# A transformer layer's expert stage: all products as three fp32r passes, row tile by row tile

## The chip, the core and the metric

The kernel runs on one core of a Trainium2 chip. The metric is the device time of one execution in microseconds (us). A core has TensorE (matmuls into PSUM), VectorE, ScalarE, GpSimd and the queues that issue DMAs; each engine works through its own instructions in order and waits on semaphores for the others. In profile rows they are PE, DVE, ACT, POOL and SP.

## The reference, cut to what matters

One layer of a hybrid attention and state-space trunk on 512 tokens of width 1024, then a mixture of experts, a gated embedding and a final norm. The change lies in the experts (and in the norm ahead of them):

```python
tok = h.reshape(-1, d)                         # h = rms_norm(x, moe_norm_w), 512 x 1024
logits = tok @ router_w + router_b             # 32 experts
top_vals, top_idx = lax.top_k(logits, 4)
gate_w = jax.nn.softmax(top_vals, axis=-1)
...
gu = lax.ragged_dot(x_sorted, w_up, group_sizes) + b_up[e_sorted]      # 1024 -> 2048
g, u = gu[:, :D_EXPERT], gu[:, D_EXPERT:]
g = jnp.minimum(g, 7.0)
u = jnp.clip(u, -7.0, 7.0)
act = (u + 1.0) * (g * jax.nn.sigmoid(1.702 * g))
out = lax.ragged_dot(act, w_down, group_sizes) + b_down[e_sorted]      # 1024 -> 1024
out = out * gate_w.reshape(-1)[order][:, None]
y = jax.ops.segment_sum(out, token_of, num_segments=n_tok)
```

Inputs and output are float32.

## The kernel before

The stages follow each other: projections, attention and the scan (to about 985 us), the router (to about 1085), the 32 experts (to about 2335), the gather of their outputs, the embedding and the final norm. All engines' programs are written out by hand, and their order is the order of the code; semaphores that only count up tie them.

An expert works on a block of 128 tokens. GpSimd gathers their rows from HBM (`fetch`, an index copy and an indirect DMA), TensorE transposes them (`turn_x`), VectorE multiplies the norm's weights in (`take_x`). The up product has 1024 rows of weights in eight row tiles of 128, and 2048 columns; it is made in two halves of 1024 columns, g and u of 512 each. Half 0 is plain fp32 products. Half 1 and the down product are made of three fp32r passes each (`mm3`): tokens and weights are split into a high part, which ScalarE writes (`ACT.Copy` into an fp32r tile, line 886), and a low part, which VectorE writes (the difference, line 1380), and the passes are high x high, high x low and low x high. The parts of one row tile of 1024 columns lie in one of four slots (`piece_hi`, `piece_lo`, in the trace `h_hi`, `h_lo`); a slot is written anew when TensorE has used it (`unit_used`). Tokens and activations are split in the same way (`x_hi`, `x_lo`, `act_hi`, `act_lo`, in the trace `w_hi`, `w_lo`).

After each up half VectorE clamps g and u out of PSUM, ScalarE takes the sigmoid of 512 columns, and VectorE joins them (`activate`, four VectorE operations of 512 columns). The activation is transposed (`turn_act`), split, and goes into the down product; ScalarE scales the result by the gate and stores it (`expert_out`, line 869). The experts overlap: a round b on TensorE is

```python
def round_of(b):
    up(b, 0)
    turn_act(b - 1)
    up(b, 1)
    turn_x(b + 1)
    down(b - 1)
```

Weights are loaded by SP: 16 loads of 512 KB for the up product and four of 1 MB for the down product, each when its place in SBUF has been read. The up loads have rows of 2 KB. All 32 experts' first blocks are computed; blocks for more than 128 tokens of an expert would follow, and none does here.

Of the kernel before, what the change touches and what calls it, by code (L numbers as in the profile page):

```python
# [15 lines left out]
P = 128  # L16
# [31 lines left out]
HALF = FF // 2  # L48
UNITS = 4
# [54 lines left out]
def up_piece(b, k):  # L104


    return b * 16 + (MOE_UNITS + k - (0 if isinstance(b, int) and b in (0, EXPERTS) else 8))


def down_piece(b, k):  # L110

    return b * 16 + (MOE_UNITS + k + (8 if isinstance(b, int) and b in (EXPERTS - 1, BLOCKS - 1) else 16))
# [30 lines left out]
def build(nc, x, p, mix_norm_w, w_in, lambda_q1, lambda_k1, lambda_q2, lambda_k2, da_head_norm_w,  # L143
# [3 lines left out]
    with ExitStack() as ctx:  # L147
# [32 lines left out]
        def bank(b, n=512, start=0):  # L180
# [126 lines left out]
        w_unit_up = [[arena[:, kb(32 * h + 8 * c):kb(32 * h + 8 * c + 8)].rearrange(  # L307
            "p (j u n) -> p j u n", j=2, u=2) for c in range(UNITS)] for h in range(2)]
        w_unit_dn = [at(64 + 8 * c, 2, D) for c in range(UNITS)]


        piece_hi, piece_lo = ([h[:, 2 * s:2 * s + 2, :] for s in range(4)] for h in (h_hi, h_lo))
        up_rows = [w_unit_up[1][k // 2][:, k % 2] for k in range(KT)]
        down_rows = [w_unit_dn[k // 2][:, k % 2, :].rearrange("p (n c) -> p n c", n=2) for k in range(KT)]
        act_hi, act_lo = w_hi[:, 0], w_lo[:, 0]
        x_hi, x_lo = w_hi[:, 1], w_lo[:, 1]
        xg, xgT = at(MOE_AT, D), at(MOE_AT + 4, KT, P)
        hidden = at(MOE_AT + 8, FF)
        y_out = at(MOE_AT + 16, D)
        g_sb, u_sb, sig_sb, t_sb = (at(MOE_AT + 20 + 2 * i, HALF) for i in range(4))  # L320
# [56 lines left out]
        (block_token_ready, xg_landed, x_turned, xt_ready, up_used, up_done, g_ready, sig_ready, hidden_own,  # L377
         act_ready, act_turned, actt_ready, act_hi_ready, x_hi_ready, x_lo_ready, down_done, y_ready, y_stored, bias_up_landed,
         bias_dn_landed) = (sem(n) for n in (
            "block_token_ready", "xg_landed", "x_turned", "xt_ready", "up_used", "up_done",  # L380
            "g_ready", "sig_ready", "hidden_own", "act_ready", "act_turned", "actt_ready",
            "act_hi_ready", "x_hi_ready", "x_lo_ready", "down_done", "y_ready", "y_stored", "bias_up_landed", "bias_dn_landed"))
        w_up_landed = [[sem(f"w_up_landed{h}{c}") for c in range(UNITS)] for h in range(2)]
        w_dn_landed = [sem(f"w_dn_landed{c}") for c in range(UNITS)]
# [14 lines left out]
        w_up_d = w_up[0].rearrange("e (c j p) (u h n) -> e h c p j u n", j=2, p=P, u=2, h=2)  # L399
        w_dn_d = w_down[0].rearrange("e (c j p) n -> e c p j n", j=2, p=P)  # L400

        PARAM_DMAS = 15
        block = ctx.enter_context(nc.Block())
# [5 lines left out]
        def _(sp):  # L409
# [54 lines left out]
            def load_up(i, half, expert):  # L464
                for c in range(UNITS):
                    if half == 0:

                        wait(sp, up_used, UNITS * (i - 1) + c + 1)
                    elif not isinstance(i, int) or i:

                        sp.wait_ge(lo_ready, up_piece(i - 1, 2 * c + 1) + 1)
                    for j in range(2):
                        sp.dma_start(w_unit_up[half][c][:, j],
                                     w_up_d[ds(expert, 1), half, c, :, j].rearrange("a p u n -> (a p) u n")
                                     ).then_inc(w_up_landed[half][c], 16)

            def load_bias_up(i, expert):
                wait(sp, up_done, 2 * i)
                sp.dma_start(bias_up[0:3, :], bup_dram[:, ds(expert * (2 * FF), 2 * FF)]
                             ).then_inc(bias_up_landed, 16)  # L480

            def load_down(i, expert):
                for c in range(UNITS):
                    if not isinstance(i, int) or i:

                        sp.wait_ge(lo_ready, down_piece(i - 1, 2 * c + 1) + 1)
                    sp.dma_start(w_unit_dn[c], w_dn_d[ds(expert, 1), c].rearrange("a p j n -> (a p) j n")
                                 ).then_inc(w_dn_landed[c], 16)
# [4 lines left out]
            sp.wait_ge(mg_projected, 2 * KT)  # L493
            sp.dma_start(w_r, router_w[0].rearrange("(k p) n -> p k n", p=P)).then_inc(w_r_landed, 16)

            sp.wait_ge(out_projected, TT)
            load_up(0, 0, 0)
            load_up(0, 1, 0)
# [8 lines left out]
            load_up(1, 0, 1)  # L507
            load_up(1, 1, 1)
            load_bias_up(1, 1)
            load_down(0, 0)  # L510
            with sp.Fori(2, EXPERTS) as i:
                load_up(i, 0, i)
                load_up(i, 1, i)
                load_bias_up(i, i)
                load_down(i - 1, i - 1)
            load_down(EXPERTS - 1, EXPERTS - 1)

            extra = sp.value_load(control[0:1, EXTRA:EXTRA + 1], min_val=0, max_val=EXTRA)
            with sp.If(extra > 0):
# [3 lines left out]
                for b in range(2):  # L523
                    e = owner_of(b)
                    load_up(EXPERTS + b, 0, e)
                    load_up(EXPERTS + b, 1, e)
                    load_bias_up(EXPERTS + b, e)
                load_down(EXPERTS, owner_of(0))
                with sp.Fori(2, EXTRA) as b:
                    e = owner_of(b)  # L530
                    load_up(b + EXPERTS, 0, e)
                    load_up(b + EXPERTS, 1, e)
                    load_bias_up(b + EXPERTS, e)
                    load_down(b + (EXPERTS - 1), owner_of(b - 1))
                load_down(BLOCKS - 1, owner_of(EXTRA - 1))


            sp.wait_ge(up_done, 2 * EXPERTS)
            with sp.If(extra > 0):
                sp.wait_ge(up_done, 2 * BLOCKS)  # L540
# [14 lines left out]
        def _(pool):  # L555
# [65 lines left out]

            pool.wait_ge(tables_ready, 1)
            for t in range(TT):
                pool.wait_ge(h2_stored[t], 16)
            fetch(0)
            with pool.Fori(1, EXPERTS) as b:
                fetch(b)
# [1256 lines left out]
```

## Time and profile before

| | |
|---|---|
| time, median of 3 runs | 2461.74 us (2461.18 to 2462.36) |
| span of the profiled execution | 2460.5 us |
| TensorE busy | 2221.8 us (90%) |
| VectorE busy | 1421.8 us (58%) |
| ScalarE busy | 959.0 us (39%) |
| GpSimd busy | 120.9 us (5%) |
| moved by DMA | 526.58 MB, 214 GB/s over the span |

Busy time counts matmuls as pipelined, with modelled ends, so a busy TensorE is not one at its peak. A plain fp32 product stands in the trace as two records, an fp32r pass as one. The weights' loads into the array (PEld) overlap with the matmuls. Times from here on are counted from the start of the span.

### The profile page before, as it was taken

What the parts mean: (1) busy time and instruction counts of PE and PEld (TensorE: products, weight loads), DVE (VectorE), ACT (ScalarE), POOL (GpSimd) and SP (SyncE); (2) the same over time, 40 slices, a digit from 0 to 9 for tenths busy, and PEclk for the clock granted to TensorE, in tenths of its full rate; (3) what the DMA queues carried; (4) which work ended last, traced back from release to release, by engine and by line L of the source; (5) the groups of instructions that cost most, each with busy time, mean ns of one, the idle gap of its engine ahead of it and who ended that gap; (6) DMA issues with size and microseconds to landing.
All of it is one profiled execution on the core that took longest, in us unless ns stands there. A gap on an engine that the chain in (4) does not pass through costs nothing.

```text
span 2460.5 us, 27486 instructions
## 1 busy us (share of the span) xinstructions
PE 2221.8 (90%) x8811; PEld 1532.9 (62%) x8876; DVE 1421.8 (58%) x1720; ACT 959.0 (39%) x1177; POOL 120.9 (5%) x141
## 2 busy tenths in 40 slices
PE   4998897979779999849999999999999999999858
PEld 3776776867545554525767667676666766667623
DVE  4666666856521110326767777676776767767542
ACT  3444244243110110114545555455554555545513
POOL 0000010100100000030000000000000000000020
PEclk9999898989889999869999999999999999999969
DMA  3225121212042220439999999999999999999540
GB/s 101 69 60 196 52 69 52 67 41 62 1 145 77 68 69 19 156 107 393 351 351 368 340 359 352 349 363 343 360 350 352 361 340 364 350 352 360 211 148 34
DMA packets 307103, 526.58 MB, mean 214 GB/s; under 512 B 17638, under 2 KB 125750, under 8 KB 307062
## 3 DMA queue, kind: packets, MB, share of 16 engines
q1 hardware_dynamic: 291776, 480.67, 56.7%
q0 software_dynamic: 7424, 25.19, 2.8%
q10 hardware_dynamic: 7862, 20.19, 2.1%
q8 instruction: 24, 0.39, 0.1%
q14 instruction: 17, 0.14, 0.0%
HBM read 496.50 MB, written 29.49 MB: 214 GB/s over the span
## 4 chain that ended last, share of the span: by engine, by line
PE 85%; DVE 7%; issue 2%; ACT 2%; DMA 2%; POOL 1%; ACTq 0%; DVEq 0%; POOLq 0%; SPq 0%
PE psum L1474 80%; PE psum L1746 1%; PE psum L1752 1%; DVE arena L1075 1%; PE psum L1594 1%; PE psum L1481 1%; POOL slots_dram L608 1%; PE psum L1641 1%; DMA arena<-y_dram,rows_u 1%; DMA arena<-in_lambda_k 0%; DVE residual L1445 0%; ACT w_hi L690 0%; ACT arena L802 0%; DVE arena L982 0%; DMA arena<-in_w_in 0%
## 5 line engine op out<-in xcount | busy, mean ns | idle before, releaser
L1474 PE MATMUL psum<-arena 128*128 128x512 f32 (+7 forms) x2384 | 865.5, 528 | 43.2 <-DVE arena L1269 13.4
L1474 PEld LDWEIGHTS psum<-arena 128*128 128x128 f32 (+1 forms) x2384 | 410.5, 196 | 467.9 <-issue 418.5
L1474 PE MATMUL psum<-h_hi,w_hi 128*128 128x512 f32 x1664 | 666.0, 400 | 7.4 <-DVE h_lo L1380 5.1
L1474 PE MATMUL psum<-h_hi,w_lo 128*128 128x512 f32 x1664 | 650.4, 391 | 0.0
L1474 PE MATMUL psum<-h_lo,w_hi 128*128 128x512 f32 x1664 | 650.0, 391 | 0.0
L1380 DVE TENSOR_TENSOR h_lo<-arena,h_hi 128x1024 fp32r<-128x1024 f32 x512 | 600.8, 1219 | 33.2 <-ACT h_hi L886 20.4
L886 ACT ACTIVATE h_hi<-arena 128x1024 fp32r<-128x1024 f32 x512 | 520.3, 1052 | 83.2 <-PE psum L1474 75.0
L1474 PEld LDWEIGHTS psum<-h_hi,w_hi 128*128 128x128 f32 x1664 | 314.0, 189 | 81.1 <-issue 16.5
L1474 PEld LDWEIGHTS psum<-h_hi,w_lo 128*128 128x128 f32 x1664 | 313.4, 188 | 66.8
L1474 PEld LDWEIGHTS psum<-h_lo,w_hi 128*128 128x128 f32 x1664 | 314.0, 189 | 65.4 <-issue 3.8
L954 DVE TENSOR_TENSOR w_lo<-arena,w_hi 128x1024 fp32r<-128x1024 f32 x80 | 100.4, 1257 | 131.4 <-ACT w_hi L690 131.1
L861 ACT ACTIVATE arena<-arena 128x512 f32<-128x512 f32 x64 | 40.5, 632 | 338.7 <-DVE arena L1396 338.7
L1396 DVE TENSOR_SCALAR arena<-psum 128x512 f32<-128x512 f32 x64 | 43.9, 686 | 181.0 <-PE psum L1474 181.0
L1376 DVE TENSOR_TENSOR w_lo<-arena,w_hi 128x1024 fp32r<-128x1024 f32 x32 | 39.2, 1225 | 151.1 <-ACT w_hi L881 151.1
L836 ACT ACTIVATE arena<-psum 128x512 f32<-128x512 f32 x16 | 9.6, 597 | 235.4 <-PE psum L1474 235.4
L869 ACT ACTIVATE arena<-psum,gate_tab 128x1024 f32<-128x1024 f32 x32 | 35.7, 1114 | 157.8 <-PE psum L1474 157.8
L690 ACT ACTIVATE w_hi<-arena 128x1024 fp32r<-128x1024 f32 x80 | 84.0, 1051 | 33.1 <-PE psum L1474 28.0
L765 ACT ACTIVATE arena<-psum 128x512 f32<-128x512 f32 x40 | 23.9, 598 | 177.2 <-PE psum L1474 177.1
L619 POOL DMA_INDIRECT arena<-h_dram,block_token x32 | 41.9, 1311 | 899.2 <-PE psum L1746 898.4
L1262 DVE TENSOR_TENSOR arena<-arena,psum 128x512 f32<-128x512 f32 x8 | 5.5, 688 | 105.9 <-ACT arena L836 94.4
L594 POOL TENSOR_TENSOR arena<-after,gdta 128x1024 f32<-128x1024 f32 x16 | 34.5, 2154 | 624.3 <-DVE gdta L1156 460.7
L1268 DVE TENSOR_TENSOR arena<-arena,psum 128x512 f32<-128x512 f32 x8 | 5.5, 689 | 94.2 <-PE psum L1474 94.2
(249 smaller groups left out, 1449.4 us busy)
## 6 DMA issues: line engine op xcount, KB each, us to landing
arena<-in_w_up SPq DMA_DIRECT2D x512, 512.0 KB, 6.6
arena<-in_w_down SPq DMA_DIRECT2D x128, 1024.0 KB, 9.1
arena<-in_w_in SPq DMA_DIRECT2D x80, 512.0 KB, 3.9
y_dram<-arena ACTq DMA_DIRECT2D x32, 512.0 KB, 5.3
arena<-in_w_ssd_branch SPq DMA_DIRECT2D x8, 1024.0 KB, 5.6
y_dram<-arena SPq DMA_DIRECT2D x1, 7680.0 KB, 23.0
arena<-in_w_attn_branch SPq DMA_DIRECT2D x8, 512.0 KB, 3.8
arena<-in_w_out SPq DMA_DIRECT2D x2, 2048.0 KB, 13.2
```

Of the source, the lines that this page charges most:

```text
L594: pool.tensor_tensor(dta_after, after[:].unsqueeze(1).broadcast_to([P, HG, P]), gdta[:, c, :].unsqueeze(2).broadcast_to([P, HG, P]), ALU.m ...
L608: pool.indirect_dma_start(slots_dram, bass.IndirectOffsetOnAxis(rows_u[:, j:j + 1], 0), slot_info[:, j, :], None).then_inc(slots_stored, 16)
L619: pool.indirect_dma_start(xg, None, h2_dram, bass.IndirectOffsetOnAxis(block_token[:], 0)).then_inc(xg_landed, 16)
L690: act.activation(w_hi[:, unit.slot], w_raw[unit.slot], ACT.Copy).then_inc(hi_ready, 1)
L861: act.activation(sig_sb, g_sb, ACT.Sigmoid, scale=ALPHA).then_inc(sig_ready, 1)
L869: act.activation(y_out, psum[:, 4 * 512:6 * 512], ACT.Copy, scale=gate_tab[:, ds(b, 1)]).then_inc(y_ready, 1)
L886: act.activation(piece_hi[slot], rows, ACT.Copy).then_inc(hi_ready, 1)
L954: dve.tensor_tensor(w_lo[:, unit.slot], w_raw[unit.slot], w_hi[:, unit.slot].bitcast(F32), ALU.subtract).then_inc(lo_ready, 1)
L1376: dve.tensor_tensor(x_lo, xgT, x_hi.bitcast(F32), ALU.subtract).then_inc(x_lo_ready, 1)
L1380: dve.tensor_tensor(piece_lo[slot], rows, piece_hi[slot].bitcast(F32), ALU.subtract).then_inc(lo_ready, 1)
L1396: dve.tensor_scalar(g_sb, bank(2 * half), LIMIT, None, ALU.min).then_inc(g_ready, 1)
L1474: return pe.matmul(o, l, r, start=start, stop=stop)
```

## The change

Every product of the experts is now made in three fp32r passes, and both halves of the up product are one.

- Up: 16 row tiles of 128 x 1024 weights (eight of g's columns and eight of u's, in turn) go through the four slots, into PSUM banks 0 to 3. Down: eight as before. Each row tile is loaded by a DMA of its own with 4 KB rows.
- ScalarE writes all 24 high parts. VectorE writes 20 low parts, GpSimd four: up tiles 3, 8 and 13 (`POOL_UP`) and down tile 5 (`POOL_DOWN`), counted from 0. TensorE and the loads wait on two counters, one for each writer.
- The clamps are over 1024 columns each; ScalarE computes Silu(1.702 g) in place of the sigmoid; VectorE joins in one operation; the factor 1/1.702 goes into the split of the activation.
- The norm's weights are multiplied into the tokens before the router and before they are stored for the gather, by a scalar_tensor_tensor in place of a tensor_scalar; `take_x` goes, and the tokens are split straight from PSUM.
- TensorE's round is up(b), turn_x(b + 1), down(b - 1), turn_act(b). On GpSimd `fetch(b + 1)` now stands after the three up tiles of b.
- The first down product's weights are loaded after the router's products; ScalarE stores an expert's output one round later.

The core of the diff:

```diff
+UP_PIECES, DOWN_PIECES = 2 * KT, KT
+POOL_UP, POOL_DOWN = (3, 8, 13), (5,)
...
+            def load_up(i, expert):
+                for n in range(UP_PIECES):
+                    if not isinstance(i, int) or i:
+                        wait_up_lo(sp, i - 1, n)
+                    sp.dma_start(w_up_part[n], w_up_d[ds(expert, 1), n // 2, n % 2].rearrange("a p n -> (a p) n")
+                                 ).then_inc(w_up_landed[n // 2], 16)
...
+            def split_up(b):                      # GpSimd
+                for i in POOL_UP:
+                    n = up_piece(b, i)
+                    pool.wait_ge(piece_hi_ready, n + 1)
+                    pool.tensor_tensor(piece_lo[i % 4], up_rows[i], piece_hi[i % 4].bitcast(F32), ALU.subtract
+                                       ).then_inc(piece_lo_pool, 1)
...
+            def experts(first, end):              # GpSimd
+                fetch(first)
+                fetch(first + 1)
+                split_up(first)
+                with pool.Fori(first + 1, end - 1) as b:
+                    split_up(b)
+                    fetch(b + 1)
+                    split_down(b - 1)
...
+            def swish(b):
+                act.wait_ge(g_ready, b + 1)
+                act.activation(g_sb, g_sb, ACT.Silu, scale=ALPHA).then_inc(sig_ready, 1)
...
+            def round_of(b, first=False, last=False):      # ScalarE
+                split_up(b, 0, 4)
+                split_act(b - 1)
+                if not first:
+                    expert_out(b - 2)
+                split_up(b, 4, 16)
+                split_down(b - 1, 0, 4)
+                if not last:
+                    split_x(b + 1)
+                split_down(b - 1, 4, 5)
+                swish(b)
+                split_down(b - 1, 5, 8)
...
+                if stage == 1:
+                    dve.wait_ge(moe_w_landed, 16)
+                    dve.scalar_tensor_tensor(out=buf[:, t % 2, :], in0=xs[:, t, :], scalar=stat[:, n, 0:1],
+                                             in1=moe_w, op0=ALU.mult, op1=ALU.mult).then_inc(xn_ready, 1)
...
             def round_of(b):                      # TensorE
-                up(b, 0)
-                turn_act(b - 1)
-                up(b, 1)
-                turn_x(b + 1)
+                up(b)
+                turn_x(b + 1, b)
                 down(b - 1)
+                turn_act(b)
```

GpSimd, the loop over the experts, before: an index copy (`block_token`) and the gather of `h2_dram`'s rows, and nothing else.

```order
L626 UNCONDITIONAL_BRANCH
L626 ISA
L614 ISA
L614 COPY block_token<-slot_token 128x1
L615 REGISTER_ALU
L619 DMA arena<-h2_dram,block_token 128x1024
```

The same loop in the changed kernel; line 666 is an up tile's low part, 673 a down tile's, `arena` the loaded weights.

```order
L680 UNCONDITIONAL_BRANCH
L680 ISA
L666 TENSOR_TENSOR h_lo<-arena,h_hi 128x1024
L665 REGISTER_ALU
L666 TENSOR_TENSOR h_lo<-arena,h_hi 128x1024
L665 REGISTER_ALU
L666 TENSOR_TENSOR h_lo<-arena,h_hi 128x1024
L99 ISA
L654 ISA
L654 COPY block_token<-slot_token 128x1
L655 REGISTER_ALU
L659 DMA arena<-h_dram,block_token 128x1024
```

Index copy and gather have moved behind three low parts, each of which waits for ScalarE's high part; down tile 5's comes after them.

VectorE in the changed kernel, the down phase of a round, from up tile 15's low part on without the four of down tiles 0 to 3: line 1473 clamps g, 1451 splits the tokens, 1456 is a low part, 1476 clamps u, 1483 joins.

```order
L1473 TENSOR_SCALAR arena<-psum 128x1024
L1450 REGISTER_ALU
L1451 TENSOR_TENSOR w_lo<-psum,w_hi 128x1024
L1455 REGISTER_ALU
L1456 TENSOR_TENSOR h_lo<-arena,h_hi 128x1024
L1476 TENSOR_SCALAR arena<-psum 128x1024
L1483 SCALAR_TENSOR_TENSOR arena<-arena 128x1024
L1455 REGISTER_ALU
L1456 TENSOR_TENSOR h_lo<-arena,h_hi 128x1024
L1455 REGISTER_ALU
L1456 TENSOR_TENSOR h_lo<-arena,h_hi 128x1024
```

Before, the place after the last down tiles held two clamps and two products of 512 columns for each half:

```order
L1396 TENSOR_SCALAR arena<-psum 128x512
L1397 TENSOR_SCALAR arena<-psum 128x512
L126 REGISTER_ALU
L1399 SCALAR_TENSOR_TENSOR arena<-arena 128x512
L126 REGISTER_ALU
L1402 TENSOR_TENSOR arena<-arena 128x512
```

Eight operations of 512 columns became three of 1024, and they now stand between down tiles 3 and 6, on both sides of tile 4, with GpSimd's tile 5 beside them.

## Rows read from the trace of the kernel before

**Rows 1.** The page: busy time, and DMA's share in 40 slices, in tenths.

```profile
PE 2221.8 (90%) x8811; PEld 1532.9 (62%) x8876; DVE 1421.8 (58%) x1720; ACT 959.0 (39%) x1177; POOL 120.9 (5%) x141
...
DMA  3225121212042220439999999999999999999540
```

**Rows 2.** Chain of waits (start, us, what) in a round; then TensorE's timeline.

```profile
1620.41 14.54 PE psum L1474 x35
...
1635.83 10.89 PE psum L1474 x48
1646.72 0.07 issue
...
1659.02 14.54 PE psum L1474 x35
...
1620.63 13.90 PE L1474 MATMUL psum<-arena 128*128 128x512 f32 x32
...
1634.36 0.59 PE L1474 MATMUL psum<-arena,ones_bf 128*128 128x512 bf16 x2
```

**Rows 3.** Windows: us, busy by engine (x instructions), clock, DMA share, GB/s.

```profile
1300.00:2100.00 800.00, 797.22 (x3058) 540.85 (x3098) 562.37 (x559) 417.58 (x433) 31.83 (x42) 1.00 0.98 353
...
1151.00:1160.00 9.00, 8.93 (x34) 6.03 (x35) 4.46 (x5) 3.51 (x5) 0.18 (x1) 1.00 1.03 409
```

**Rows 4.** Timelines of ScalarE and VectorE: start, us, operation, idle before it.

```profile
1638.60 1.06 ACT L886 ACTIVATE h_hi<-arena 128x1024 fp32r<-128x1024 f32 x1 [0.30 <-PE psum L1474]
1639.96 1.06 ACT L886 ACTIVATE h_hi<-arena 128x1024 fp32r<-128x1024 f32 x1 [0.30 <-PE psum L1474]
...
1622.89 1.06 ACT L881 ACTIVATE w_hi<-arena 128x1024 fp32r<-128x1024 f32 x1 [0.86 <-ACT arena L869]
...
1086.18 4.62 DVE L1380 TENSOR_TENSOR h_lo<-arena,h_hi 128x1024 fp32r<-128x1024 f32 x4
```

**Rows 5.** Timelines of GpSimd and VectorE in the scan stage.

```profile
323.06 1.90 POOL L594 TENSOR_TENSOR arena<-after,gdta 128x1024 f32<-128x1024 f32 x1 [318.76 <-DVE gdta L1156]
...
323.21 1.77 DVE L1120 COPY gconv<-conv_col 128x16 f32 x1 [0.24 <-DVE gdta L1156]
...
381.28 2.58 POOL L594 TENSOR_TENSOR arena<-after,gdta 128x1024 f32<-128x1024 f32 x1 [19.35 <-PE psum L1474]
...
438.59 2.09 DVE L954 TENSOR_TENSOR w_lo<-arena,w_hi 128x1024 fp32r<-128x1024 f32 x1 [2.43 <-ACT w_hi L690]
```

**Rows 6.** Timelines of GpSimd (index copy, gather) and TensorE (its first transposes).

```profile
1076.27 1.01 POOL L619 DMA_INDIRECT arena<-h_dram,block_token  x1 [0.84 <-POOL block_token L614]
...
1080.71 1.94 PE L1746 MATMUL psum<-ident,arena 128*128 128x128 f32 x8 [6.02 <-DMA arena<-h_dram,block_token]
...
1083.45 0.98 POOL L619 DMA_INDIRECT arena<-h_dram,block_token  x1 [2.52 <-PE psum L1746]
1088.58 1.13 POOL L614 COPY block_token<-slot_token 128x1 uint32 x1 [4.16 <-DMA arena<-h_dram,block_token]
...
1185.18 1.33 POOL L619 DMA_INDIRECT arena<-h_dram,block_token  x1 [29.77 <-PE psum L1746]
1193.37 0.18 POOL L614 COPY block_token<-slot_token 128x1 uint32 x1 [6.85 <-DMA arena<-h_dram,block_token]
```

**Rows 7.** VectorE: the router's normalisation (timeline) and the last norm's form (groups).

```profile
1004.88 0.75 DVE L974 TENSOR_SCALAR arena<-residual,stat 128x1024 f32<-128x1024 f32 x1
...
L1465 DVE SCALAR_TENSOR_TENSOR arena<-residual,stat,arena 128x1024 f32<-128x1024 f32 x4 | 5.1, 1286 | 0.1
```

**Rows 8.** The end of the expert stage: timeline of TensorE, then the chain of waits.

```profile
2277.25 1.02 PE L1474 MATMUL psum<-arena 128*128 128x512 f32 x2
...
2321.51 12.76 PE psum L1474 x48
```

**Rows 9.** TensorE ahead of the second expert: timeline, and a window as in rows 3.

```profile
1116.50 0.89 PE L1474 MATMUL psum<-arena 128*128 128x512 f32 x1 [3.09 <-DVE arena L1365]
...
1115.00:1120.00 5.00, 3.50 (x5) 1.55 (x6) 3.88 (x5) 3.52 (x4) 0.43 (x1) 0.69 1.04 400
```

More of the change, by code:

```diff
@@ L462, in _ @@
             load_merge(KT - 1)
[L464 to L475, printed above, removed]
+            def load_up(i, expert):
[4 more added lines that the diff above has]
+                                 ).then_inc(w_up_landed[n // 2], 16)
             def load_bias_up(i, expert):
-                wait(sp, up_done, 2 * i)
+                wait(sp, up_done, i)
                 sp.dma_start(bias_up[0:3, :], bup_dram[:, ds(expert * (2 * FF), 2 * FF)]
@@ L883, in split_piece @@
+                act.activation(x_hi, psum[:, 6 * 512:8 * 512].rearrange("p (k t) -> p k t", t=P), ACT.Copy
+                               ).then_inc(x_hi_ready, 1)
             def split_piece(number, slot, rows):
-                act.wait_ge(unit_used, max(MOE_UNITS, number - 3) if isinstance(number, int) else number - 3)
-                act.activation(piece_hi[slot], rows, ACT.Copy).then_inc(hi_ready, 1)
-            def split_up(b, start):
-                for k in range(start, start + 4):
-                    act.wait_ge(w_up_landed[1][k // 2], 32 * (b + 1))
-                    split_piece(up_piece(b, k), k % 4, up_rows[k])
@@ new lines, in split_piece, with split_up, split_down @@
+                act.activation(piece_hi[slot], rows, ACT.Copy).then_inc(piece_hi_ready, 1)
+            def split_up(b, start, end):
+                for i in range(start, end):
+                    if i % 2 == 0:
+                        act.wait_ge(w_up_landed[i // 2], 32 * (b + 1))
+                    split_piece(up_piece(b, i), i % 4, up_rows[i])
+            def split_down(b, start, end):
+                for k in range(start, end):
+                    if k % 2 == 0:
+                        act.wait_ge(w_dn_landed[k // 2], 32 * (b + 1))
+                    split_piece(down_piece(b, k), k % 4, down_rows[k])
@@ L913, in experts @@
                 split_x(first)
-                sigmoid_half(first, 0)
-                split_up(first, 4)
-                sigmoid_half(first, 1)
-                round_of(first + 1)
-                with act.Fori(first + 2, end) as b:
+                split_up(first, 4, 16)
+                split_x(first + 1)
+                swish(first)
+                round_of(first + 1, first=True)
+                with act.Fori(first + 2, end - 1) as b:
                     round_of(b)
+                round_of(end - 1, last=True)
@@ L1405, in _, with split_up, split_down @@
-            mine = Own(dve, hidden_own)
+                                  ).then_inc(piece_lo_dve, 1)
+            def split_up(b, start, end):
+                for i in range(start, end):
+                    if i not in POOL_UP:
+                        split_piece(up_piece(b, i), i % 4, up_rows[i])
+            def split_down(b, start, end):
+                for k in range(start, end):
+                    if k not in POOL_DOWN:
+                        split_piece(down_piece(b, k), k % 4, down_rows[k])
@@ L1407, in experts, with round_of @@
+            def round_of(b, last=False):
+                split_up(b, 0, 4)
+                split_act(b - 1)
+                split_up(b, 4, 16)
+                split_down(b - 1, 0, 4)
+                take_g(b)
+                if not last:
+                    split_x(b + 1)
+                split_down(b - 1, 4, 5)
+                take_u(b)
+                split_down(b - 1, 5, 6)
+                join(b)
+                split_down(b - 1, 6, 8)
             def experts(first, end):
-                take_x(first)
+                split_up(first, 0, 4)
@@ L1426, in experts @@
+                take_g(first)
+                split_x(first + 1)
+                take_u(first)
+                join(first)
                 with dve.Fori(first + 1, end - 1) as b:
-                    mine.round(b, first + 1, 4)
                     round_of(b)
-                    take_x(b + 1)
-                mine.rounds(end - first - 2)
-                round_of(end - 1)
-                take_act(end - 1)
-                split_down(end - 1, 0)
-                split_down(end - 1, 4)
+                round_of(end - 1, last=True)
```

295 lines of the change are left out of this document (145 added, 150 removed).

## The prediction

> **What bounds the kernel now.** I read the page first, for the engine that is busy over the whole span, then the chain of waits and the timelines of one round of the expert stage, since nearly all of the diff lies there. TensorE is busy 90% of the span, and from the 19th slice on DMA's digits are nines [rows 1]. Two resources look full there, so the question is which ends last. In the 800 us from 1300 to 2100 TensorE is busy 797.22 us at a clock of 1.00, and the chain is TensorE alone [rows 2, 3]. The DMA share there is 0.98, but its 353 GB/s are no ceiling: 409 GB/s move where down loads, 4 KB packets, run with a backlog [rows 3]. TensorE sets the round; DMA follows.
>
> A round (one expert's up half 0, transposes of the previous activation, up half 1, transposes of the next tokens, the previous expert's down product) is 38.61 us, from 1620.41 to 1659.02 [rows 2]. It is made of 13.73 us of plain fp32 products (1620.63 to 1634.36) [rows 2], two blocks of 48 fp32r passes (10.89 us and 0.07 behind it; the second is alike) [rows 2], two transposes of about 0.8, and six bias products of 0.215 us. A row tile, six passes, takes 1.36 us: ScalarE's high parts, paced by TensorE, start 1.36 apart [rows 4].
>
> **Part 1, the passes.** The 13.73 us become 48 more passes at 10.97. That is 2.76 less, a floor of 38.61 - 2.76 = 35.85 us for a round. Over 30 rounds this alone would be 83 us.
>
> **Part 2, the splitting.** 24 row tiles instead of 16 are split per round. ScalarE: 24 at 0.95 to 1.06, two splits of about 1.0, Silu of 1024 columns about 1.05 and the scaling with its store, about 2.0 (line 869's own 1.1 and 0.86 behind it) [rows 4]: 29 us, under 35.85, off the path. VectorE: four low parts take 4.62 us in a row, 1.22 for one alone and 1.14 for each further one [rows 4], so 22.8 us for 20; two splits, two clamps and one product of 1024 columns, about 1.2 each, 6 us: 28.8 us. It would be off the path too, if GpSimd's four tiles cost it nothing.
>
> **They do.** The trace has GpSimd operations of this shape in the scan stage. They last 1.90 us, and 2.58 when VectorE's low part started first (381.28) [rows 5]. The other way round a copy of 16 columns lasts 1.77 us and ends with GpSimd's (323.21 + 1.77 = 324.98; 323.06 + 1.90 = 324.96), and a low part that takes 1.22 alone lasts 2.09 behind one (438.59) [rows 5]. So an operation of either engine holds the other, and GpSimd's takes about 1.7 us out of a VectorE that is always ready. 28.8 + 4 x 1.7 = 35.6, just below the floor: VectorE is full, but not the bound on average. What counts is where it is late. Operations with a PSUM operand (the clamps, the splits of activation and tokens) I take as free of GpSimd; no row shows one beside it, and if they were held too, a round would be about 1 us longer. The Trainium skill, page "SBUF — State Buffer", section "Who interferes with whom", has the rule that a VectorE operation with two SBUF inputs and a GpSimd operation that reads SBUF exclude each other for the whole instruction, while VectorE with at most one SBUF input goes free; the trace agrees with the first half (1.90 against 2.58, 1.22 against 2.09), and the second is the choice just made, which no run here shows yet.
>
> I lay the round out from its start U. In the up phase TensorE wants tile i at U + 1.36 i; a slot is free again four tiles later. High part: 0.20 us after TensorE releases the slot, 1.06 long; low part 1.22 after that [rows 4]. VectorE's tiles come 0.4 to 1 us early; GpSimd's tile 8 waits for VectorE's tile 7, ends at about U + 10.6 and is wanted at 10.9. So no stall in the up phase. In the down phase it is otherwise. With V the start of the transposes of the next tokens: down tile 4 is split at V + 4.7, the clamp of u ends at 5.8, GpSimd has tile 5 from 5.65 to 7.55, and the product that joins g and u, two SBUF operands, can't run before; it ends at 8.65, low part 6 at 9.8, and TensorE wants it at 8.95. **Stall of 0.85 us per round.**
>
> **Part 3, the gather of the next tokens.** Before, its only company on GpSimd was the index copy, and it is issued right behind the transposes that read its buffer, nearly a round ahead of its own: at 1185.18, landed by 1193.37 [rows 6]. Now it stands behind GpSimd's third up tile and in front of transposes that follow the up product of the same round. Tile 9 is released at U + 13.6, high part 13 ends at 14.85, GpSimd has it from 14.95 to 16.85. Then VectorE's tile 14 is waiting, holds the copy of the index to 18.0 (the copy takes 0.18 us alone and 1.13 among VectorE's low parts [rows 6]), and the gather starts 0.8 us after the copy, as at 1076.27: U + 18.8. Landing: 4.4 us with idle queues (1076.27 to TensorE's 1080.71), 5.1 for the second (1083.45 to 1088.58), 8.2 with a backlog (1185.18 to 1193.37) [rows 6]. TensorE is ready at U + 22.6 (16 tiles of 1.36, four biases). The stall is 0.6 with idle queues and up to 4.4 with a backlog. Between the two: a load of 512 KB takes 1.28 us at 409 GB/s and one is issued per tile, every 1.36 us, so about one transfer stands ahead of the gather; I estimate 4.8 + 1.1 = 5.9 us. **Stall of 2.1 us per round.**
>
> Bandwidth doesn't end it: at 409 GB/s the 13.6 MB of a round (353 GB/s times 38.6 us) take 33.3 us.
>
> **Round:** 35.85 + 0.85 + 2.1 = 38.8 us, 0.2 more than now.
>
> **Part 4, around the rounds.** The router's normalisation takes a second tensor: 1.28 in place of 0.75 us (line 1465's form), four times on TensorE's path [rows 7]: +2.1. The first expert runs wholly at the half clock until it has warmed up, and TensorE idles over 4 us before the second while clamp, Silu and product run one after the other: about +1.2 in all against now. The end gains: from the last expert's first up product to the end of its down product it takes 57.0 us (2277.25 to 2321.51 + 12.76 = 2334.27) [rows 8]. In the new order it is 22.6 + 11.5 + 0.85 + 0.8 + 2.7 + 11.5 = 50.0: -7.0, where the half clock after the short idle may cost 0.7 again. So -6.3.
>
> **Sum** against the profiled 2460.5: 30 x 0.19 = +5.7 (the round itself is read to 0.03 us at best); +2.1; +1.2; -6.3; together +2.7, a span of 2463. The median of the runs, 2461.74, is 1.2 above the profiled span; both move together. I predict **2464 us**. Anything within 4.9 us (0.2%) is about what a measurement can't tell from no change.
>
> **Rivals.**
> - *The queue is empty when the gather comes.* For it: the average need is 353 GB/s against 409. Against: the loads of the next expert are issued tile by tile in just that phase. Stall 0.6: round 37.3, 30 x 1.3 = 39 less than now, with the rest (-3.0) 2420 us. Chance 0.22.
> - *The engines don't hold each other,* because the operands differ from the scan's. Against: three kinds of rows. No stall in the down phase, the gather 1.1 us earlier: round 36.85, 2406 us. Chance 0.08.
> - *The gather meets a backlog, as the one at 1185.18 does, which stands for all in the rounds now* [rows 6] (slower). Stall 3.5 to 4.4; it decides from the point on where the clock falls too: after the idle 3.09 us before 1116.50, with transposes ahead, TensorE was granted 0.69 on average in 1115 to 1120, and a record of a plain product took 0.89 in place of 0.43 [rows 9]. Without the clock 40.2 us a round, 2507 us; with it in each round 0.9 more, 2534 us. Chance 0.20.
> - *GpSimd's subtraction is slower than 1.90 us* with two full inputs and an fp32r output, which no row shows. Bounds: 1.90 and 2.58. At +0.35 the gather, down tile 5 and all behind it come later, together about 1.0 us a round: 2494 us; at +0.7, 2524. Chance 0.15.
>
> On that last price the Trainium skill, page "GPSIMD Engine Reference", section "Performance versus the Vector engine", states 4497 ns for a tensor_tensor of 2048 fp32 columns, about 2.25 us for 1024 (an estimate by that page). The sum by it would be 2494 us; by the row it is 2464, and the row, from this chip and this length, has the say.
>
> **How the numbers follow.** The forecast (stall 1.7 to 2.5, 2452 to 2476) has 0.30, of which 0.08 is faster by over 0.2%, 0.14 within, 0.08 slower. 0.05 is left for something else that is late, slower. Faster: 0.08 + 0.22 + 0.08 = 0.38; within 0.2%: 0.14; slower: 0.08 + 0.20 + 0.15 + 0.05 = 0.48. The range takes the empty queue and most of the backlog: 2410 to 2530.
>
> **What would show it.** The plain fp32 products are gone from the rounds, and 144 passes stand in each. The distance from one gather to the next is the round: 38.8, not 37 or 40. TensorE's waits name the gather's landing about 2 us in each round and VectorE's low part (the tile after GpSimd's in the down phase) under 1. GpSimd's index copies last about 1 us, VectorE's longest low parts 2 to 3 us. The clock stays at 9 or 10 tenths; digits of 8 would mean the third rival. I am wrong at the root if TensorE waits for neither, if it waits on weights, or if GpSimd's subtraction isn't near 1.90.

## The result, and the profile after the change

| | before | after |
|---|---|---|
| median time | 2462.05 us (2461.18 to 2462.62) | 2610.36 us (2608.26 to 2612.79) |
| span of the profiled execution | 2460.5 us | 2610.4 us |
| TensorE's mean granted clock | 1.00 in the rounds | 0.94 in the rounds |

The changed kernel is slower: ratio 1.0606, 95% interval 1.0591 to 1.062. The forecast was 2464 us, no change, with a range of 2410 to 2530. It was wrong.

The page of the changed kernel, against [rows 1] (busy time, then the span in 40 slices, in tenths):

```profile
PE 2216.3 (85%) x9324; PEld 1669.1 (64%) x9388; DVE 1613.0 (62%) x1656; ACT 1238.0 (47%) x1401; POOL 466.9 (18%) x269
...
PE   5997898897699998288889898989898989898948
...
PEclk9998998998899998589999999999999999999969
DMA  3224221220233303578887878797979797878550
```

The expert stage was a row of nines for TensorE and DMA; now neither is full. Something makes both wait. The window 1300 to 2100 (as in [rows 3]) and the waits of TensorE in it (us in total, times, longest):

```profile
1300.00:2100.00 800.00, 710.93 (x3036) 563.89 (x3071) 612.44 (x461) 537.76 (x520) 231.96 (x112) 0.94 0.84 315
...
PE psum L1825 <- DMA arena<-h_dram,block_token: 77.4, 18, 4.5
PE psum L1553 <- DVE h_lo L1456: 8.8, 18, 0.6
```

Eighteen rounds, and in each the transposes of the next tokens (line 1825) wait for the gather, 4.3 us on the mean. From here it is one timeline of one round, first GpSimd, with U = 1603.67 the first pass of the up product. This round takes 44.1 us; the mean of 30 is 43.47.

```profile
1603.77 2.54 POOL L666 TENSOR_TENSOR h_lo<-arena,h_hi 128x1024 fp32r<-128x1024 f32 x1 [6.48 <-ACT h_hi L950]
1611.93 2.69 POOL L666 TENSOR_TENSOR h_lo<-arena,h_hi 128x1024 fp32r<-128x1024 f32 x1 [5.62 <-ACT h_hi L950]
1618.87 2.52 POOL L666 TENSOR_TENSOR h_lo<-arena,h_hi 128x1024 fp32r<-128x1024 f32 x1 [4.24 <-ACT h_hi L950]
1621.32 1.19 POOL L654 COPY block_token<-slot_token 128x1 uint32 x1
1623.32 1.13 POOL L659 DMA_INDIRECT arena<-h_dram,block_token  x1 [0.81 <-POOL block_token L654]
1638.95 2.40 POOL L673 TENSOR_TENSOR h_lo<-arena,h_hi 128x1024 fp32r<-128x1024 f32 x1 [14.50 <-ACT h_hi L950]
1647.86 2.53 POOL L666 TENSOR_TENSOR h_lo<-arena,h_hi 128x1024 fp32r<-128x1024 f32 x1 [6.51 <-ACT h_hi L950]
...
1667.41 1.13 POOL L659 DMA_INDIRECT arena<-h_dram,block_token  x1 [0.81 <-POOL block_token L654]
```

The gather starts at U + 19.65; TensorE gets it at 1631.20, 7.9 us later:

```profile
1625.94 0.81 PE L1553 MATMUL psum<-arena,ones_bf 128*128 128x512 bf16 x3
1631.20 1.97 PE L1825 MATMUL psum<-ident,arena 128*128 128x128 f32 x8 [4.45 <-DMA arena<-h_dram,block_token]
1632.82 0.78 PE L1553 MATMUL psum<-h_hi,w_hi 128*128 128x512 f32 x1
1633.40 0.63 PE L1553 MATMUL psum<-h_lo,w_hi 128*128 128x512 f32 x1
```

Behind the wait TensorE is slow: the eight transposes take 1.62 us (1631.20 to 1632.82) instead of 0.79, and passes start 0.43 apart instead of 0.23. The granted clock is 0.50 from 1631 to 1636: 1.2 GHz instead of 2.4. The clock falls once in every round; in 8 of the 30 it falls so late that the transposes take little longer than usual. Why the landing takes 7.9 us is to be seen on the DMA queue (SyncE's issues, `SPq` in the rows: all sixteen in one row, then the first four and the other twelve; then two windows with the columns of [rows 3]):

```profile
1604.12 19.98 SPq L507 DMA_DIRECT2D arena<-in_w_up  x16
...
1604.12 2.69 SPq L507 DMA_DIRECT2D arena<-in_w_up  x4
...
1609.10 14.99 SPq L507 DMA_DIRECT2D arena<-in_w_up  x12
...
1603.70:1612.00 8.30, 8.30 (x39) 6.85 (x38) 5.86 (x6) 7.00 (x7) 2.61 (x2) 1.00 0.86 262
1612.00:1634.00 22.00, 17.49 (x75) 13.87 (x75) 15.39 (x12) 12.48 (x12) 7.39 (x4) 0.91 1.03 413
```

Four loads of 512 KB go out within 2.7 us, and ScalarE's store of an expert's output, another 512 KB, follows them at 1606.15. Until 1612 the queues move only 262 GB/s. The other twelve loads come 1.33 us apart (11 steps from 1609.10 to 1623.76) and need 1.27 us each at 413 GB/s, so the backlog hardly shrinks: from 1612 on, eleven us ahead of the gather, the queues are full. When the gather is issued, at 1623.32, four loads are on their way (issued from 1618.27 to 1622.63, landed from 1624.76 to 1629.08). The first load of the sixteen landed in 4.0 us, the later ones in 6.4 (median of the window 1612 to 1623).

Last VectorE, in the down phases of this round and the next: the join (line 1483) and a clamp (1476) and, in the up phase, the activation's split (1445).

```profile
1639.25 3.19 DVE L1483 SCALAR_TENSOR_TENSOR arena<-arena 128x1024 f32<-128x1024 f32 x1
...
1649.10 1.22 DVE L1445 SCALAR_TENSOR_TENSOR w_lo<-psum,w_hi 128x1024 fp32r<-128x1024 f32 x1 [0.99 <-ACT w_hi L939]
...
1682.47 3.04 DVE L1483 SCALAR_TENSOR_TENSOR arena<-arena 128x1024 f32<-128x1024 f32 x1
```

The join starts beside GpSimd's tile 5 (1638.95 to 1641.35), ends 1.09 us behind it and lasts 3.19 us (1.22 where GpSimd does nothing beside it, as a later experiment shows): held. The split 1445, with a PSUM operand, lies wholly within GpSimd's 1647.86 to 1650.39 and takes its usual 1.22 us: not held.

**Where the 149.9 us between the spans lie**, by TensorE's timelines: up to the second expert's first pass 8.9 (1116.50 became 1125.37); 30 rounds 143.4 (from 38.69 to 43.47 us on the mean); the end of the expert stage -5.1 (57.1 became 52.0 us); behind it 2.7. The rounds decide.

### The profile page after: what moved, and what is told of

It reads as the page before. It is cut to its first block, busy times and chain, and to the rows that moved or that the text cites. A ratio compares the mean times of both kernels' runs of the same rounds, so it can differ in the third digit from the quotient of the medians.

```text
span 2610.4 us, 29814 instructions
## 1 busy us (share of the span) xinstructions
PE 2216.3 (85%) x9324; PEld 1669.1 (64%) x9388; DVE 1613.0 (62%) x1656; ACT 1238.0 (47%) x1401; POOL 466.9 (18%) x269
## 4 chain that ended last, share of the span: by engine, by line
issue 43%; PE 35%; POOL 10%; DVE 7%; DMA 2%; ACT 2%; ACTq 0%; POOLq 0%; DVEq 0%; SPq 0%
PE psum L1553 32%; POOL h_lo L666 6%; POOL block_token L654 1%; POOL arena L659 1%; DVE residual L1524 1%; DVE h_lo L1456 1%; DVE arena L1154 1%; DMA arena<-h_dram,block_token 1%; PE psum L1720 1%; PE psum L1673 1%; PE psum L1560 1%; POOL slots_dram L648 1%; DMA arena<-in_lambda_k 0%; ACT w_hi L753 0%; ACT arena L865 0%
## 5 line engine op out<-in xcount | busy, mean ns | idle before, releaser
L950 ACT ACTIVATE h_hi<-arena 128x1024 fp32r<-128x1024 f32 x768 | 803.6, 1059 | 270.0 <-PE psum L1553 250.4
L1553 PE MATMUL psum<-h_hi,w_hi 128*128 128x512 f32 x2176 | 896.6, 412 | 23.6 <-DVE h_lo L1456 15.4
L1456 DVE TENSOR_TENSOR h_lo<-arena,h_hi 128x1024 fp32r<-128x1024 f32 x640 | 816.7, 1330 | 158.4 <-ACT h_hi L950 158.0
L1553 PE MATMUL psum<-h_lo,w_hi 128*128 128x512 f32 x2176 | 868.5, 399 | 0.0
L1553 PE MATMUL psum<-h_hi,w_lo 128*128 128x512 f32 x2176 | 866.0, 398 | 0.0
L1553 PEld LDWEIGHTS psum<-h_hi,w_hi 128*128 128x128 f32 x2176 | 424.4, 195 | 146.9 <-DVE h_lo L1456 28.6
L1553 PEld LDWEIGHTS psum<-h_lo,w_hi 128*128 128x128 f32 x2176 | 422.7, 194 | 85.9 <-issue 3.8
L1553 PE MATMUL psum<-arena 128*128 128x512 f32 (+7 forms) x1360 | 417.3, 476 | 39.0 <-DVE arena L1348 13.4
L1553 PEld LDWEIGHTS psum<-arena 128*128 128x128 f32 (+1 forms) x1360 | 214.1, 198 | 227.8 <-issue 187.6
L666 POOL TENSOR_TENSOR h_lo<-arena,h_hi 128x1024 fp32r<-128x1024 f32 x96 | 247.4, 2577 | 527.0 <-ACT h_hi L950 527.0
L673 POOL TENSOR_TENSOR h_lo<-arena,h_hi 128x1024 fp32r<-128x1024 f32 x32 | 77.0, 2405 | 441.0 <-ACT h_hi L950 441.0
```

The lines of the kernel that those rows point to most:

```text
L666: pool.tensor_tensor(piece_lo[i % 4], up_rows[i], piece_hi[i % 4].bitcast(F32), ALU.subtract).then_inc(piece_lo_pool, 1)
L673: pool.tensor_tensor(piece_lo[k % 4], down_rows[k], piece_hi[k % 4].bitcast(F32), ALU.subtract).then_inc(piece_lo_pool, 1)
L950: act.activation(piece_hi[slot], rows, ACT.Copy).then_inc(piece_hi_ready, 1)
L1456: dve.tensor_tensor(piece_lo[slot], rows, piece_hi[slot].bitcast(F32), ALU.subtract).then_inc(piece_lo_dve, 1)
L1553: return pe.matmul(o, l, r, start=start, stop=stop)
```

## The experiments

Ratios are against the kernel before, run beside each. A single time has no interval.

**The theory**: the gather's place behind GpSimd's up tiles costs the wait, and the wait costs the clock; the order on VectorE in the down phase costs another 1 us; the product as passes is as cheap as forecast. **Rivals**: GpSimd's subtractions themselves, and the lock that they put on VectorE, are the loss; or the gather is slow in the midst of the rounds whatever the queue holds.

### The gather ahead of the up tiles

```diff
 with pool.Fori(first + 1, end - 1) as b:
-    split_up(b)
     fetch(b + 1)
+    split_up(b)
     split_down(b - 1)
```

> The changed kernel with one line moved: on GpSimd the gather of the next tokens stands ahead of the three up tiles of a round, not behind them. Theory (the gather, issued late, is waited for and lets the clock fall): its wait of 4.4 us goes, with it the fall of the clock (together about 6 us of a round of 43.5). What is left late is the down tile behind GpSimd's, 1.0 to 1.4 us with GpSimd's 2.4 us per tile. Round 37.0 (36.8 to 37.4), time 2610 - 31 x 6.5 = 2409 (2400 to 2425). Rival (GpSimd's slow tiles and the hold on VectorE cost most of it): the round stays over 40 us, time over 2500.

Measured: 2423.0 us (2421.58 to 2426.55), ratio 0.9842 (0.9826 to 0.9859). The waits of TensorE in 1300 to 2100, and the window:

```profile
PE psum L1553 <- DVE h_lo L1456: 12.3, 22, 0.6
...
1300.00:2100.00 800.00, 782.66 (x3527) 620.76 (x3569) 704.16 (x539) 622.93 (x603) 268.21 (x131) 1.00 0.97 366
```

One line moved, and 187 us are gone, 6.2 per round: the gather isn't waited for any more, the clock is 1.00, and GpSimd has all its tiles (268 us busy). So the tiles are not the main loss; the gather's place is. It still takes 7.5 us to land here (median of 22), but nobody waits. What is left is a late low part in each round: 48 passes and a bias product of the down phase take 12.45 to 12.49 us.

### All low parts on VectorE

```diff
-POOL_UP, POOL_DOWN = (3, 8, 13), (5,)
+POOL_UP, POOL_DOWN = (), ()
```

> The changed kernel with all 24 low parts of a round on VectorE and none on GpSimd; the gather is then free of them too. VectorE's own sum: 24 x 1.14 + 6 = 33.4 us in a round of 35.85. Theory: no wait for the gather, no hold; the round is the 35.85 us of the passes plus at most 1 us where VectorE's clamps and product stand ahead of down tiles: 35.9 to 36.8, time 2375 to 2405, faster than with the gather moved alone. Rival (VectorE can't carry all tiles, its work comes in bursts): round over 37.5, slower than with the gather moved alone.

Measured: 2401.57 us (2400.68 to 2402.55), ratio 0.9751 (0.9735 to 0.9768). A round is 36.47 us. VectorE is busy 742.65 of the 800 us and a low part is late by 0.4. It makes every low part itself, and the kernel is faster than with GpSimd's help: four tiles save VectorE 4 x 1.14 us and cost it the time that it is held.

### GpSimd's low parts of 16 columns

```diff
-pool.tensor_tensor(piece_lo[i % 4], up_rows[i], piece_hi[i % 4].bitcast(F32), ALU.subtract
+pool.tensor_tensor(piece_lo[i % 4][:, :, 0:8], up_rows[i][:, :, 0:8], piece_hi[i % 4].bitcast(F32)[:, :, 0:8], ALU.subtract
```

The same at the down tile; the order stays that of the change.

> The changed kernel, in which GpSimd's four low parts are written for 16 of their 1024 columns alone, the rest left out; every wait and the order stay. Theory: the order alone still makes the gather late. It starts about 2.9 us earlier (tile 13's 2.5 us and the copy held behind VectorE), near U + 16.5, and with the backlog it lands 7.9 later: wait 1.2 to 2 us, too short for the clock to fall; no late down tile. Round 37.0 to 38.0, time 2405 to 2440. If the backlog is smaller by then, the wait is under 1 and the round 36.5. Rival (the order is innocent, the length of GpSimd's work is the whole cause): no wait for the gather at all, round 35.9.

Measured: 2409.21 us, one run. The gather now starts at U + 16.24 (1603.38 to 1619.62) and lands 7.5 us later, and the wait is 0.8 to 1.0 us a round (1.2 to 2 were expected), with no fall of the clock from 1300 to 2100:

```profile
PE psum L1825 <- DMA arena<-h_dram,block_token: 17.4, 21, 1.0
```

3.4 us earlier, and the wait is 3.5 shorter. A round is 36.8 us. The landing hardly changed, so GpSimd's subtractions are not what makes it long.

### The wait kept, TensorE kept busy

```diff
+def fill(b):
+    pe.wait_ge(actt_ready, b)
+    for n in range(18):
+        mm(bank(6 + n % 2), x_hi[:, n % KT, :], x_hi[:, 0:4, :], True, True)
```

It stands between the up product and the transposes.

> The changed kernel with 18 added passes of 512 columns (4.1 us) between the up product and the transposes of the next tokens, in the time in which TensorE waits for the gather; their result goes nowhere. Theory: the clock stays at full speed. That gives back what the half clock costs: 0.83 us at the transposes and about 1.0 (up to 1.9) in the down product; the wait itself is filled, not shortened. Round 43.5 - 1.9 = 41.6 (41.0 to 42.2), time 2550 (2535 to 2570). Rival (the half clock is hidden, since VectorE's late tile would make TensorE wait anyway): the round shortens by under 1 us, time over 2580.

Measured: 2559.08 us (2557.74 to 2561.38), ratio 1.0392 (1.0375 to 1.0409). TensorE around the filled wait:

```profile
1566.31 4.47 PE L1553 MATMUL psum<-w_hi 128*128 128x512 f32 x18
1571.01 1.09 PE L1825 MATMUL psum<-ident,arena 128*128 128x128 f32 x8 [0.23 <-DMA arena<-h_dram,block_token]
```

The transposes are as late as in the change, but take 0.85 us, and the clock stays at 1.00 in 1300 to 2100. (2610.36 - 2559.08) / 30 = 1.7 us a round is what the clock costs; (2559.08 - 2423.0) / 30 = 4.5 is the wait itself. Together they are the 6.2 of the first experiment.

### The join behind the last down tiles

```diff
-split_down(b - 1, 5, 6)
+split_down(b - 1, 5, 8)
 join(b)
-split_down(b - 1, 6, 8)
```

Once on the kernel with the gather ahead, once on the one with all low parts on VectorE.

> The gather ahead of GpSimd's up tiles, as in e1, and the join behind down tiles 6 and 7; GpSimd keeps its four tiles. In e1 down takes 12.45 to 12.49 us, 1.05 over 11.43. Theory (the stall is the one that the prediction named at tile 6: the join waits for GpSimd's tile 5 and tile 6 waits for the join): down comes to 11.4 to 11.9, the round from 37.2 to 36.2 to 36.7, the time to 2390 to 2410 us. Rival: low part 6 itself is held until GpSimd's tile 5 ends, so that the join's place hardly counts; then down stays above 12.2 and the time at 2418 to 2426 us.

> All low parts on VectorE, as in e2, and the product that joins g and u behind down tiles 6 and 7 in place of in front of tile 6. In e2 a round is 36.47 us: up 22.10, transposes 0.65 to 0.79, down 11.92 in place of the 11.43 that two bias products and 48 undisturbed passes take. Theory: what is left over the floor in e2 is low part 6, which stands behind the clamps, the split of the tokens and the join. Then down comes to 11.4 to 11.5, the round to 35.9 to 36.1, and the time to 2383 to 2392 us. Rival: VectorE is full (742.65 of 800 us) and late wherever the join stands; then the loss only moves to tile 7 or to the next transposes and the time stays at 2398 to 2404 us.

Measured, with GpSimd's tiles: 2395.33 us (2393.6 to 2396.52), ratio 0.973 (0.9713 to 0.9746). The 48 passes with one bias take 11.58 to 11.61 instead of 12.49 us. So 0.9 of the 1.05 was the join in front of low part 6, and it was late because it was held: without the hold it would have ended 1.8 us sooner, in time for tile 6 (an estimate from its 3.0 us against 1.22).

Without them: 2380.27 us (2376.25 to 2382.74), a little under the 2383 to 2392 expected, ratio 0.9672 (0.9656 to 0.9688), the fastest version of this study, 3.3% under the kernel before run beside it (2462.87 us). Its window and VectorE's timeline in the down phase:

```profile
1300.00:2100.00 800.00, 800.00 (x3715) 651.40 (x3715) 758.09 (x650) 647.58 (x627) 44.90 (x44) 1.00 1.00 381
...
1579.36 1.22 DVE L1476 TENSOR_SCALAR arena<-psum 128x1024 f32<-128x1024 f32 x1
1580.50 3.49 DVE L1456 TENSOR_TENSOR h_lo<-arena,h_hi 128x1024 fp32r<-128x1024 f32 x3
1583.90 1.22 DVE L1483 SCALAR_TENSOR_TENSOR arena<-arena 128x1024 f32<-128x1024 f32 x1
```

TensorE is busy 800.00 of 800 us. A round is 35.77 us (1551.64 to 1587.41), and the trace names no wait of it. DMA's share is 1.00 as well: VectorE (758), TensorE and the queues are all nearly full.

### Half of each up load, and half of the up loads

```diff
-sp.dma_start(w_up_part[n], w_up_d[ds(expert, 1), n // 2, n % 2]...
+sp.dma_start(w_up_part[n][0:64], w_up_d[ds(expert, 1), n // 2, n % 2, 0:64]...
```

> The changed kernel, but from the third expert on only rows 0 to 63 of each up row tile of 128 are loaded (packets of 4 KB as before); the other rows keep earlier weights, so half of the up weights' loading is left out. Order of the gather as in the change. In the changed kernel the gather is issued 19.65 us after the round's start and lands 7.7 to 7.9 us later, TensorE waits 4.4 to 4.6 and its clock halves in each round. Theory (a backlog of the loads makes the landing long): the loads in front of the gather are half, it lands in 4.4 to 5.3 us, the wait falls to 1.2 to 2.0 us, the clock mostly stays at 1.00, the round is 38.0 to 39.3 us, the time 2450 to 2490 us. Rival (the landing is long for another reason, GpSimd's own path or the gather's small packets): it stays at 7 us or more, the round at 43 us, the time above 2580 us.

Measured: 2552.57 us, one run. The gather lands in 5.8 to 6.7 us, TensorE waits 2.9 on the mean (55.4 us in 19 waits), and the round is 41.5 us on the mean: neither theory's number. The window tells why this isn't a free queue; the second line is that of the next experiment:

```profile
1300.00:2100.00 800.00, 733.05 (x3217) 576.34 (x3216) 643.59 (x485) 561.42 (x544) 242.79 (x118) 0.97 0.82 229
...
1300.00:2100.00 800.00, 762.99 (x3418) 599.64 (x3459) 691.72 (x522) 602.66 (x584) 256.91 (x124) 1.00 0.72 249
```

Loads into 64 partitions move less (229 GB/s) in more of the queues' time (0.82). Halving the bytes took next to nothing off the queues' busy share (0.84 in the changed kernel), so this run says nothing of free queues. In the next one tiles 8 to 15 of the up weights are loaded with 3 rows:

```diff
+sp.dma_start(w_up_part[n][0:P if n < 8 else 3], w_up_d[ds(expert, 1), n // 2, n % 2, 0:P if n < 8 else 3]...
```

> The changed kernel, but from the third expert on the up row tiles 8 to 15 are loaded with 3 rows instead of 128 (the rest keeps earlier weights, so nearly half of the up weights' loading is left out); tiles 0 to 7 are loaded whole, as in the change. In the half loads of e7 packets of both queues took 240 ns in place of 163, so that run doesn't tell what a gather on free queues takes. Here the last whole load is issued some 10 us before the gather, and none stands in front of it. Theory (the backlog of the loads makes the difference between 4.4 to 5.1 us, as with the first two gathers, and 7.7 to 7.9): it lands in 4.4 to 5.1 us, TensorE waits 1.3 to 2.2 us a round instead of 4.4; with the clock at 1.00 the round is 38.5 to 39.3 us and the time 2460 to 2490, with the clock still falling in each round 40.4 to 41.2 and 2515 to 2540. Rival (it is the gather itself in the midst of the rounds): it stays at 6 us or more, the round above 41.5 and the time above 2545 us.

Measured: 2462.95 us, one run.

```profile
1607.93 1.13 POOL L665 DMA_INDIRECT arena<-h_dram,block_token  x1 [0.81 <-POOL block_token L660]
...
1612.47 1.09 PE L1831 MATMUL psum<-ident,arena 128*128 128x128 f32 x8 [1.12 <-DMA arena<-h_dram,block_token]
```

Landed in 4.5 us, and the round is 38.5 us (1573.95 to 1612.47). The gather starts where it does in the change (U + 19.65), with the same work on GpSimd and VectorE beside it. Only the loads in front of it are gone, and with them 3.3 us of landing, and then the clock's fall. The backlog is the cause, not GpSimd, not a hold by VectorE and not the gather in itself. It rests on one run, but its 30 rounds agree: the landings are 4.2 to 4.8 us, against 7.5 to 7.9 in the rounds of the change (8.3 once).

### Other operands for GpSimd's subtraction

```diff
-pool.tensor_tensor(piece_lo[i % 4], up_rows[i], piece_hi[i % 4].bitcast(F32), ALU.subtract
+pool.tensor_tensor(piece_lo[i % 4], up_rows[i], piece_hi[i % 4].bitcast(F32)[:, :, 0:1].broadcast_to([P, 2, 512]), ALU.subtract
```

At the down tile both inputs are broadcast. All on the kernel with the gather ahead.

> As e1 (gather ahead), with GpSimd's low parts on other operands, which leaves these low parts wrong: in the three up tiles the second input is one column spread over 512 by a broadcast, in the down tile both inputs are; the output is fp32r as before. In e1 GpSimd's down tile takes 2.41 us on the mean (and 2.59 for the up tiles, part of that behind VectorE), the scan's operation, with two broadcast inputs and another output type, 1.90. Theory: it is the full inputs that cost the 0.5 us; then the down tile takes about 1.9 and the up tiles 1.9 to 2.2 where VectorE isn't ahead. Rival: the fp32r output or the subtraction costs it; then the down tile stays at 2.4. The time hardly matters: 2405 to 2425 us.

Measured: 2401.16 us, one run, a little under the 2405 to 2425 expected; the round is 36.5 instead of 37.2 us. GpSimd's groups in 1300 to 2100:

```profile
L666 POOL TENSOR_TENSOR h_lo<-arena,h_hi 128x1024 fp32r<-128x1024 f32 x66 | 134.3, 2034 | 311.7 <-ACT h_hi L950 311.7
L673 POOL TENSOR_TENSOR h_lo<-arena,h_hi 128x1024 fp32r<-128x1024 f32 x21 | 39.8, 1894 | 236.9 <-ACT h_hi L950 236.9
```

1894 ns in place of 2408, with the output still fp32r. The up tiles, with one full input and one broadcast, take 1.90 as well where VectorE isn't ahead. It is the second full input that costs 0.5 us, and with GpSimd's operations shorter by it a round is 0.7 us shorter.

## Why the prediction was wrong, step by step

**Held.** Part 1: the floor was 35.85 us; the round without stalls is 35.77. No plain fp32 product is left in the rounds, and the 83 us that the passes save are there: in the version that has nothing else late 30 rounds go from 38.69 to 35.80 us on the mean, 87 us. That its whole time is 82.6 less (2462.87 to 2380.27) lies nearer to 83 by chance. DMA doesn't end the round, though 381 GB/s leave it little. Of Part 2: the engines hold each other, and the PSUM operations go free (1.22 us inside GpSimd's 2.53). The Trainium skill, page "SBUF — State Buffer", section "Who interferes with whom", says that a VectorE instruction with at most one SBUF input, outside its 2-port modes, doesn't contend with GpSimd; these 1.22 us bear it out, which no row of before could. The late low part at down tile 6 was foreseen at 0.85 us a round and is about 0.9 where nothing hides it, by the mechanism named (the join behind tile 5).

**The step that failed is the landing in Part 3.** "About one transfer stands ahead of the gather": 4.8 + 1.1 = 5.9 us; it is 7.5 to 7.9, with four loads on their way. The two rates were right for most of the phase (a load per 1.33 us, 1.27 to move it). What they leave out is the backlog at its start, which rates so near to each other don't work off. A load waits for a low part, not for TensorE. In the round shown VectorE had the first three low parts of the up product ready at 1604.05 (1599.43 + 4.62, down tile 7 and these three). The first loads stood behind SyncE's wait for the end of the down product (its load of the bias, issued at 1603.20), and then three went out in a row, with the store and the fourth behind them:

```profile
1599.43 4.62 DVE L1456 TENSOR_TENSOR h_lo<-arena,h_hi 128x1024 fp32r<-128x1024 f32 x4
...
1603.20 0.27 SPq L524 DMA_DIRECT2D arena<-bdn_dram  x1
```

That the backlog starts here is read from the timeline; no run changes this order. The experiment with 3 rows in tiles 8 to 15 leaves this start and takes away the later loads, which keep the backlog up, and the landing is 4.5. [Rows 6] had the right value, 8.2 with a backlog, and it was priced as a rival at 0.20 instead of being the forecast. It was no single case: in 1300 to 2100 the kernel before issued 21 gathers, and their median landing (last number) was 7.9 us, with queues that moved 353 GB/s of a possible 409; there nobody waited for them.

```profile
arena<-h_dram,block_token POOLq DMA_INDIRECT x21, 7.9
```

**GpSimd's subtraction.** Taken at 1.90 from [rows 5], whose operation has two broadcast inputs. It is 2.40 alone, which is +0.5, between the two prices of the fourth rival (+0.35 and +0.7). The gather starts at U + 19.65 instead of 18.8. And the up phase has a stall, where the forecast had none: its 96 passes take 22.28 us against 21.9 undisturbed. GpSimd's tile 8 ends at U + 10.95 instead of 10.6, and TensorE's weight load waits for it:

```profile
1614.68 0.19 PEld L1553 LDWEIGHTS psum<-h_hi,w_hi 128*128 128x128 f32 x1 [0.26 <-POOL h_lo L666]
```

The Trainium skill, page "GPSIMD Engine Reference", section "Performance versus the Vector engine", gives 4497 ns for 2048 columns, 2.25 for 1024 as an estimate: nearer than the row, which was of another form.

**The clock.** Priced at 0.9 us in the third rival and left out of the forecast. It costs 1.7 us a round (up to 0.8 in the transposes, the rest in the first passes of the down product). It comes with the long wait: behind one of 1.1 us, without the backlog, the clock stays, behind 2.9 with the half loads it falls in some rounds (0.97 over the window), and behind 4.4 in every round.

The stall is then 4.4 instead of 2.1 (landing +1.95, start +0.85, and TensorE ready 0.48 later), the clock 1.7 instead of 0, the up phase 0.4, with the late tile as foreseen: 2.3 + 1.7 + 0.4 = 4.4 over the 38.8 of the forecast, 43.2; measured 43.47, and the last 0.3 is not attributed. The third and the fourth rival came true together, and they were priced one at a time. Even the third alone reached out of the range at its own upper bound: 35.85 + 0.85 + 4.4 + 0.9 = 42.0 us a round, 2560 us, but it was priced at the lower one, 3.5, and the range ended at 2530.

**Part 4.** Forecast +2.1 and +1.2 up to the second expert, measured +8.9: 3.0 up to the router's tables, 1.1 in the tokens' split (the +1.2 by luck: it was put on a first expert at the half clock, and the granted clock is 1.00 from 1098 to 1120), 0.9 because the first index copy is held beside VectorE, and 3.9 because the first gather too meets loads, three that SP issues at 1079.30 when VectorE has made the first low parts:

```profile
1079.30 2.60 SPq L507 DMA_DIRECT2D arena<-in_w_up  x3
...
1088.50 1.94 PE L1825 MATMUL psum<-ident,arena 128*128 128x128 f32 x8 [10.83 <-DMA arena<-h_dram,block_token]
```

The gather started at 1080.16: 8.3 us, where [rows 6] has 4.4. That is the same kind of error a second time. The end gained 5.1 of the 6.3, and 2.7 of it went again behind the stage, where the transposes of the embedding wait for loads that are queued behind the last down weights.

Of the list of what would show it, the wait of 4.4 us for 2 and the round of 43.5 point at the third rival, and GpSimd's 2.40 at the fourth. The clock's sign failed: digits of 8 were to mean the third rival, and the page has only nines in the rounds, since a fall for some us in each leaves a mean of 0.94.

## What to carry to other kernels

A small transfer that someone waits for must be priced by what the queue holds at its own time, so find out what releases the loads (here low parts that were made ahead) and what holds them together (here SyncE's own order), not their mean rate; if the kernel before has the same transfer in each round, take its landing from there. And issue it as early as its buffer allows, since one line's place was worth 187 us. An idle of 4.4 us on TensorE cost 1.7 more where the clock fell behind it. Work given to GpSimd was a loss here, since it lay beside VectorE's operations with two SBUF inputs; and a price for it is to be taken from a row with the same operands. Where two rivals share a cause, price them together too.

## What the runs showed of the hardware beyond what was expected

- A gather of 128 rows of 4 KB, from its issue until TensorE has it: 4.2 to 4.8 us without a backlog, 7.5 to 7.9 us in the changed kernel's rounds, with full queues.
- GpSimd's operation on 1024 columns: 1.89 to 1.90 with one or both inputs broadcast, 2.40 with two full ones. The output's type made no difference (1.90 with f32, 1.89 with fp32r).
- GpSimd's copy of one column lasts 1.19 us where VectorE is in a row of low parts (0.18 alone), as [rows 6] had it at 1.13: even a tiny operation waits about as long as one of VectorE's low parts lasts.
- Loads into 64 of 128 partitions with the same packet size: 229 GB/s at a share of 0.82, against 315 at 0.84 in the changed kernel, which loads all 128.
- With loads of 4 KB rows, 381 GB/s over 800 us didn't slow TensorE: it was busy all of them. What the larger packets alone bring wasn't measured.
